# Weight places and prefetch order for the experts of a hybrid decoder layer: seven single gate-up places and a third down place

## The reference, cut to what matters

```
x = x + gate1 * (merged @ w_o)
h = RMSNorm(x) * (1 + scale2) + shift2
# top-1 group of 4, then top-2 of its 8 experts: each token goes to 2 of 32 experts
gate = h @ w_gate[e]          # 1024 x 256 for each expert
up   = h @ w_up[e]            # 1024 x 256
act  = silu(gate) * up * combine[e]
x = x + gate2 * sum_e(act @ w_down[e])     # 256 x 1024
y = RMSNorm(x) * final_norm_w
```

## Time and profile before

| | before |
|---|---|
| median of 3 runs | 1465.02 us (1462.16 to 1473.55) |
| the profiled execution: its own time | 1467.18 us |
| the profiled execution: span of the trace | 1465.4 us |
| granted TensorE clock, mean | 0.949 |
| PE busy | 1346.7 us (92%) |
| DVE busy | 695.8 us (47%) |
| ACT busy | 257.8 us (18%) |
| POOL busy | 146.3 us (10%) |
| bytes moved by DMA | 250.87 MB, mean 171 GB/s |

### The profile page before, as it was taken

The page is one execution under the profiler, slowest core; times in us unless marked ns, Lnnn a source line. Parts: engine busy times, 40 slices in busy tenths (PEclk is TensorE's granted clock), DMA queues, the critical chain, the costliest instruction groups (busy, mean ns, idle before and its releaser), DMA issues. The chain is left out here.

```text
span 1465.4 us, 19419 instructions
## 1 busy us (share of the span) xinstructions
PE 1346.7 (92%) x7097; PEld 968.5 (66%) x7097; DVE 695.8 (47%) x1415; ACT 257.8 (18%) x554; POOL 146.3 (10%) x278
## 2 busy tenths in 40 slices
PE   5999999999999999999989998999999898888784
PEld 2787667788787787676767776788878632222233
DVE  1434677555667675310105566775567611111125
ACT  2201112112222531110112121510001300000001
POOL 0223100000000000222210003000001211111111
PEclk7899999999999999999999997899999888999995
DMA  9463223313313323555561110512236499999945
GB/s 361 155 137 94 98 73 124 121 58 116 115 58 121 103 60 127 180 170 189 187 217 60 41 30 30 219 58 72 86 107 271 187 375 427 424 424 423 409 161 183
DMA packets 61440, 250.87 MB, mean 171 GB/s; under 512 B 10058, under 2 KB 19690, under 8 KB 52234
## 3 DMA queue, kind: packets, MB, share of 16 engines
q1 hardware_dynamic: 40978, 184.26, 34.3%
q10 hardware_dynamic: 10264, 44.97, 8.6%
q0 software_dynamic: 10112, 20.47, 4.1%
HBM read 234.47 MB, written 22.91 MB: 176 GB/s over the span
## 5 line engine op out<-in xcount | busy, mean ns | idle before, releaser
L350 PE MATMUL psum<-arena 128*128 128x272 f32 x1792 | 423.3, 394 | 1.0 <-DVE arena L1903 1.0
L350 PEld LDWEIGHTS psum<-arena 128*128 128x128 f32 x1792 | 339.0, 190 | 80.9 <-issue 6.7
L362 PE MATMUL psum<-arena 128*128 128x272 f32 x1064 | 249.3, 393 | 2.2 <-DVE arena L2078 1.9
L362 PEld LDWEIGHTS psum<-arena 128*128 128x128 f32 x1064 | 199.8, 189 | 51.7 <-issue 9.7
L1255 PE MATMUL psum<-arena 128*128 128x272 f32 x512 | 122.8, 397 | 0.0
L2541 PE MATMUL psum<-arena 128*64 128x512 f32 x512 | 115.6, 603 | 2.7 <-DVE arena L2640 2.7
L1255 PEld LDWEIGHTS psum<-arena 128*128 128x128 f32 x512 | 96.2, 190 | 25.9 <-DVE arena L1380 3.6
L2541 PEld LDWEIGHTS psum<-arena 128*64 128x64 f32 x512 | 35.9, 136 | 71.2 <-issue 71.2
L2562 PE MATMUL psum<-arena 128*64 128x512 f32 x256 | 69.8, 694 | 1.2 <-DVE arena L2629 1.2
L1380 DVE TENSOR_TENSOR arena<-arena,psum 128x272 f32<-128x272 f32 x16 | 7.0, 439 | 132.1 <-ACT arena L1332 123.9
L1574 PE MATMUL psum<-arena 128*128 128x272 f32 x256 | 64.8, 407 | 2.9 <-PEq L206 2.9
(11 more groups left out here) (374 smaller groups left out, 1433.4 us busy)
## 6 DMA issues: line engine op xcount, KB each, us to landing
arena<-in_weights SPq DMA_DIRECT2D x153, 512.0 KB, 4.3
arena<-in_w_gu SPq DMA_DIRECT2D x32, 2048.0 KB, 17.6
arena<-in_w_down ACTq DMA_DIRECT2D x28, 1024.0 KB, 17.2
arena<-in_weights ACTq DMA_DIRECT2D x16, 512.0 KB, 4.1
arena<-in_pages_k POOLq DMA_DIRECT2D x40, 128.0 KB, 3.3
arena<-in_x SPq DMA_DIRECT2D x2, 2176.0 KB, 13.8
arena<-in_pages_v SPq DMA_DIRECT2D x32, 128.0 KB, 3.0
arena<-in_pages_v POOLq DMA_DIRECT2D x32, 128.0 KB, 3.3
```

Of the source, the lines that this page charges most:

```text
L350: mm = pe.matmul(out[:, h, :], lhsT=w_of(n, c), rhs=act[:, c, h * HALF:(h + 1) * HALF], start=(c == 0), stop=(c == DC - 1))
L362: mm = pe.matmul(out, lhsT=w[:, c * P:c * P + P], rhs=x[:, c, :], start=(c == 0), stop=(c == 3))
```

## The change: what it does

- The gate-up weights get seven places for single experts instead of three for pairs. The first six are the halves of the old ones; the seventh is at `a_x`, where `xT` stands. Expert `j` goes to place `j % 7`; from `j` = 7 on it is loaded when `gate_up((j-7)//2)` is done.
- Expert 4 is loaded when the rows have been turned (`s_row_ps`), expert 5 when `h2_rows` is written; neither waits for gather 0 any more.
- `xT` is written to a new DRAM tensor `x_mid` by ACT, behind the last row of `h2_rows` (2176 KB). SP waits for it (`s_xmid`) and for gather 0 and loads expert 6 into its place. Behind `gate_up(13)` SP reads `x_mid` back, and DVE waits for that (`s_xback`) ahead of `residual(0)`.
- The down weights get a third place. All three begin 192 floats lower than before, and pairs 0 and 1 are loaded when `w_o`'s pair `v` = 1 is done instead of `v` = 0, pair 2 by SP behind expert 6. ACT issues pair `p+2` in its step `p` instead of pair `p+1`, behind the same `down(p-1)`.
- Small tables of the router move to addresses that nothing else uses then.

```diff
@@ -2103,16 +2103,19 @@
...
                 "dma_may_start"))
-            gath, scat, wdn_full = (s_gath, s_gath1), (s_scat, s_scat1), (s_wdn, s_wdn1)
-            wgu_full = (s_wgu, s_wgu1, sem("wgu_loaded2"))
-            GU = 3
-            GU_USES = [len(range(k, NP, GU)) for k in range(GU)]
+            gath, scat = (s_gath, s_gath1), (s_scat, s_scat1)
+            wdn_full = (s_wdn, s_wdn1, sem("wdown_loaded2"))
+            GU, DN = 7, 3
+            wgu_full = (s_wgu, s_wgu1) + tuple(sem(f"wgu_loaded{i}") for i in range(2, GU))
+            GU_USES = [len(range(k, 2 * NP, GU)) for k in range(GU)]
+            DN_USES = [len(range(k, NP, DN)) for k in range(DN)]
+            s_xmid, s_xback = sem("x_spilled_and_back"), sem("x_is_back")
+            x_mid = nc.dram_tensor("x_mid", [P, DC, NT], F32).ap()

...
             W_GU = 2 * DC * FF
-            w_gu = [(A.at(a_q, W_GU), A.at(a_q + W_GU, W_GU)), (A.at(a_ring, W_GU), A.at(a_ring + W_GU, W_GU)),
-                    (A.at(a_h, W_GU), A.at(a_w - 192 - W_GU, W_GU))]
-            w_dn = [A.at(a_w, 2, 2 * D), A.at(a_w + 4 * D, 2, 2 * D)]
+            w_gu = [A.at(at, W_GU) for at in (a_q, a_q + W_GU, a_ring, a_ring + W_GU, a_h, a_w - 192 - W_GU, a_x)]
+            w_dn = [A.at(a_w - 192 + 4 * D * k, 2, 2 * D) for k in range(DN)]
             a_e = a_q + 8192
@@ -2159,19 +2162,21 @@
...
             tmp32 = A.at(a_r + 1200, 2, NR, NE)
-            rank = A.at(a_r + 1520, 2 * NR)
+            rank = A.at(a_param + PARAM_AT["conv_prev"][0] + 64, 2 * NR)
             p2 = A.at(a_r + 1530, NR)
             mx = A.at(a_r + 1567, 16)
-            tabf = A.at(a_r + 1583, NP)
-            pick = A.at(a_r + 1600, 2, 2 * NR, NE)
-            slot_of = A.at(a_r + 2240, 2 * NR, CAP)
+            tabf = A.at(a_param + PARAM_AT["conv_prev"][0] + 80, NP)
+            a_dead = a_const + CONST_AT["after"][0]
+            assert a_dead + 4 * NR * NE + 2 * NR * CAP <= a_const + CONST_AT["iota"][0]
+            pick = A.at(a_dead, 2, 2 * NR, NE)
+            slot_of = A.at(a_dead + 4 * NR * NE, 2 * NR, CAP)
             xn11 = A.at(a_r + 2240, DC, NEW)
             pre = A.at(a_r + 2240 + 2 * NR * CAP, NR, NE)
-            wtab = A.at(a_r + 2400 + 2 * NR * CAP, NP)
+            wtab = A.at(a_param + PARAM_AT["conv_prev"][0] + 96, NP)
             wcol = A.at(a_param + PARAM_AT["conv_prev"][0], 2, NR)
...
             rounds_i = A.at(a_keep + 20, 1).bitcast(I32)
-            rows11 = A.at(a_xb + DC * NT - 2 * D, 4, D)
+            rows11 = A.at(a_w - 192 - 4 * D, 4, D)
             assert T_O % RING + 3 < RING and T_END - T_O == RING
@@ -2210,8 +2215,8 @@
...
                     mm.then_inc(w_used, 2)
-                    if v == 0:
-                        pe.wait_ge(w_used, T_O + 2)
+                    if v == 1:
+                        pe.wait_ge(w_used, T_O + 4)
                         pe.sem_inc(s_dn, 2)
@@ -2291,6 +2296,7 @@
...
                     rows_out(i)
+                act.dma_start(x_mid, xT).then_inc(s_xmid, 16)
                 act.wait_ge(s_gi, 1)
@@ -2460,29 +2466,51 @@
...
             def _(sp):
-                def gate_up_in(r, p):
-
-                    sp.wait_ge(s_gu, r * NP + (p if p >= GU else (2, 1, 1)[p]))
+                def gate_up_in(r, j):
+
+                    last = max(k for k in range(j, 2 * NP, GU))
+                    sp.wait_ge(s_gu, r * NP + (3 + (j - GU) // 2 if j >= GU else max(last // 2 + 3 - NP, 1)))
+                    sp.dma_start(w_gu[j % GU], ins["w_gu"][j]).then_inc(wgu_full[j % GU], 16)
+
+                def down_in(r, p):
+                    sp.wait_ge(s_dn, r * NP + (2, 1, 1)[p])
                     for e in range(2):
-                        sp.dma_start(w_gu[p % GU][e], ins["w_gu"][2 * p + e]).then_inc(wgu_full[p % GU], 16)
-
-                def down_in(r, p):
-                    sp.wait_ge(s_dn, r * NP + (p + 1))
-                    for e in range(2):
-                        sp.dma_start(w_dn[p % 2][:, e, :], ins["w_down"][2 * p + e]).then_inc(wdn_full[p % 2], 16)
+                        sp.dma_start(w_dn[p][:, e, :], ins["w_down"][2 * p + e]).then_inc(wdn_full[p], 16)

...
                     gate_up_in(r, 0)
+                    gate_up_in(r, 1)
                     down_in(r, 0)
...
                     sp.wait_ge(w_used, T_END)
-                    gate_up_in(r, 1)
+                    gate_up_in(r, 2)
+                    gate_up_in(r, 3)
+                    sp.wait_ge(s_row_ps, NR)
+                    gate_up_in(r, 4)
+                    for k, n in enumerate((2, 1, 1, 1)):
+                        sp.wait_ge(s_h2w[k], 16 * n)
+                    gate_up_in(r, 5)
                     sp.wait_ge(s_slot, 1)
...
                     sp.wait_ge(gath[0], r * (8 * NP) + 16)
-                    for p in range(2, NP):
-                        gate_up_in(r, p)
+                    sp.sem_inc(s_passed, 1)
+                    sp.wait_ge(s_xmid, r * 16 + 16)
+                    sp.sem_inc(s_passed, 1)
+                    sp.wait_ge(s_sq11, DC)
+                    sp.wait_ge(s_xs, DC - 1)
+                    sp.wait_ge(s_xs7, 1)
+                    sp.wait_ge(s_xn, 1)
+                    gate_up_in(r, 6)
+                    sp.wait_ge(s_wtab, 1)
+                    down_in(r, 2)
+                    for j in range(GU, 2 * NP):
+                        gate_up_in(r, j)
+                    sp.wait_ge(s_gu, r * NP + (3 + max(range(GU - 1, 2 * NP, GU)) // 2))
+                    sp.dma_start(xT, x_mid).then_inc(s_xmid, 16)
+                    sp.wait_ge(s_xmid, r * 16 + 32)
+                    sp.sem_inc(s_passed, 1)
+                sp.sem_inc(s_xback, 1)

@@ -2532,11 +2560,12 @@
...
                     pe.wait_ge(s_xsb, r * NP + (p + 2))
-                    pe.wait_ge(wgu_full[p % GU], r * (32 * GU_USES[p % GU]) + (p // GU * 32 + 32))
+                    for j in (2 * p, 2 * p + 1):
+                        pe.wait_ge(wgu_full[j % GU], r * (16 * GU_USES[j % GU]) + (j // GU * 16 + 16))
                     pe.wait_ge(s_act, r * NP + (p + 1))
...
                         for e in range(2):
-                            wv = w_gu[p % GU][e].rearrange("p (o c f) -> p c o f", o=2, c=DC)
+                            wv = w_gu[(2 * p + e) % GU].rearrange("p (o c f) -> p c o f", o=2, c=DC)
                             at = c * P + CAP * e
@@ -2553,14 +2582,14 @@
...
                     pe.wait_ge(s_asb, r * NP + (p + 1))
-                    pe.wait_ge(wdn_full[k], r * (16 * NP) + (p // 2 * 32 + 32))
+                    pe.wait_ge(wdn_full[p % DN], r * (32 * DN_USES[p % DN]) + (p // DN * 32 + 32))
                     pe.wait_ge(s_yo, r * NP + (p + 1))
...
                                 mm = pe.matmul(psum[CAP * e:CAP * e + CAP, 4 + h, :], lhsT=actT[:, k, at:at + CAP],
-                                               rhs=w_dn[k][:, e, f * D + h * 512:f * D + h * 512 + 512],
+                                               rhs=w_dn[p % DN][:, e, f * D + h * 512:f * D + h * 512 + 512],
                                                start=(f == 0), stop=(f == 1))
@@ -2599,17 +2628,17 @@
...
                 def down_in(r, p):
-                    act.wait_ge(s_dn, r * NP + (p + 1))
+                    act.wait_ge(s_dn, r * NP + p)
                     for e in range(2):
-                        act.dma_start(w_dn[p % 2][:, e, :], ins["w_down"][2 * p + e]).then_inc(wdn_full[p % 2], 16)
+                        act.dma_start(w_dn[p % DN][:, e, :], ins["w_down"][2 * p + e]).then_inc(wdn_full[p % DN], 16)

...
                         act.activation(sil[:, k, :], psum[:, 2 + k, 0:FF], ACT.Silu).then_inc(s_silu12, 1)
-                        if 1 <= p < NP - 1:
-                            down_in(r, p + 1)
+                        if 1 <= p < NP - 2:
+                            down_in(r, p + 2)
                         act.wait_ge(s_aps, r * NP + (p + 1))
@@ -2793,6 +2822,7 @@
...
                 rows_added(4)
+                dve.wait_ge(s_xback, 1)
                 residual(0)
...
                 dve.wait_ge(s_yt, 3)
```

## The result

| | before | changed |
|---|---|---|
| median (11 runs each, same chip) | 1465.51 us | 1482.01 us |
| lowest to highest | 1460.81 to 1473.55 us | 1475.58 to 1485.26 us |
| ratio | | 1.0103, 95% interval 1.0087 to 1.0120 |
| profiled execution: time, span | 1467.18, 1465.4 us | 1485.26, 1483.6 us |

The change costs about 1%, where no change (+5 us) was forecast, and the time lies outside the range.

What follows compares the result with a forecast made beforehand. It took full DMA engines in the expert stage as the bound, reaching PE through gathers. Start +7 and end -2, the rest nothing, gave +5 us on 1465.02, a median of 1470 us; range 1454 to 1478.

Steps and rivals of the forecast that it cites:

- DMA is full and PE waits for gathers: Expert stage: the 16 DMA engines are full, and PE waits for token-row gathers, 35.6 us in 11 waits, not weights.
- Places as depth gain nothing in the pace: Expert stage: seventh place and third down place leave the pace at 16.9 us a pair; costed at nothing.
- The start, 7 us, bounds 0 to 9: Stage start: 6.43 MB ahead of gather 0 makes it land later, so the stage starts 7 us later.
- A late start is carried through unchanged: Expert stage: it repeats itself with the start's shift of 7 us, each trigger keeping its distance to the pairs.
- The way back of `x`: Reading x back behind gate_up(13): needed some 50 us on, so DVE never waits; can only hold up gather 15.
- The end, -2: Last pairs: 5 us less DMA ahead of gather 14 removes turn_x(14)'s 2.46 us wait; -2 us, bounds 0 and -3.5.
- A (turns): Rival at gather 0: engines serve queues in turn, so it lands some 1.3 us later; 1464 us; chance 0.12.
- B: Rival for the stage: bytes moved decide, so filling the gap gains; 1457 us, at most down to 1450; chance 0.19.
- C: Rival from gather 4 on: added places put more in flight, gathers land later; 1485 to 1499 us; chance 0.09.

Runs made afterwards that it cites:

- e4: Kernel before with only POOL's order changed: scatter p-4 instead of p-3 behind gather p, so gathers are issued earlier; ratio 0.9982.
- e7: Against the kernel before: six single gate-up places and three down places, no x out and back, experts 4 and 5 behind gather 0; ratio 1.0050.
- e9: Against the kernel before: six single gate-up places, two down places, gather 0 first, no x out and back; as fast, to 0.04%.
- e11: Changed kernel without the seventh place and without x out and back; early experts 4 and 5 and third down place stay; ratio 1.0049.
- e2: Kernel before in its old places, only expert 4 loaded when rows are turned and expert 5 when they are written; 1479.9 us, ratio 1.0071.
- e3: Changed kernel with expert 4 loaded behind the rows' writes, like expert 5; 1477.6 us.
- e5: Changed kernel with POOL's order changed so that the gather goes ahead of the scatter; 1470.9 us.
- e15: Changed kernel with experts 4 and 5 and the write of x issued behind gather 0's issue, by POOL's semaphore; last down 290.6 us behind w_o's end.
- e1: Changed kernel with experts 4 and 5 and the write of x moved behind gather 0's landing; 1475.8 us.
- e14: Against the kernel before: six gate-up, three down places, gather before scatter, no x, step-11 down load skipped, experts 4 and 5 at gather 0's issue; 1466.1 us, 0.9981.

## Why the prediction was wrong

1. *DMA is full and PE waits for gathers.* Right as a reading: 12 waits for gathers in the changed kernel, none for weights. Wrong as a cause, by e4: remove the gathers' waits and the same 35 us turn up at the down weights.
2. *Places as depth gain nothing in the pace.* Right to 0.2 us in 169. "I cost this at nothing" was wrong for the end: where the start is on time the third down place costs 7.7 us (e7 against e9), through one gather. In e11, which has the early experts and the third down place, its price did not add to the late start's (e11 against e2: 284.1 and 284.3); that the stock is filled while PE waits for gather 0 is the likely reason, not a shown one.
3. *The start, 7 us, bounds 0 to 9.* **This is the step that failed**: measured 11.8, with the rows that expert 4 holds up, and gather 1, put at 2 us together at most, between the 7 and the bound of 9. That the bytes ahead of gather 0 delay it was right, and the sum agrees with e3 (6.9), but in part by luck: by the reading behind it gather 0 would have landed last, and in e3 it landed 3.8 us ahead of expert 5. I counted all 6.43 MB as flowing from 1164 on, "since whatever of it goes earlier pushes bytes of the rows behind it". What was missed: expert 5 and gather 0 are issued on the landing of these rows, and expert 4, with `x` behind it, held the last block up by 8 us (10.8 instead of 2.8; without `x`, in e2, 7.9), so gather 0 was issued 6.4 us later. Transfers that are chained by a landing don't share a sum of bytes. Taking expert 4 away from the rows gives 4.9 us back (e3).
4. *A late start is carried through unchanged.* Right to 0.9 us: 11.8, 10.9, 11.0. It holds only while PE waits for gathers: with the gather ahead, 10.4 us at the start are 3.9 at the end (e5).
5. *The way back of `x`.* Landed 12.5 us behind its issue, no wait of DVE: right.
6. *The end, -2.* Wrong in sign: from `gate_up(13)` to the last `down` 43.8 us, before 42.3. Expert 31 alone in the queue did not help gather 14, which took about as long as before and kept its wait (2.32), now with a slow `down` behind it (5.35 us).

By its own terms the sum should have been 11.8 + 0.7 = 12.5 instead of 5 (0.7 is the end's 1.5 less the 0.8 that the shift lost on the way to pair 13). Its upper bound has a slip of 1 us: 1465 and 9 are 1474, not 1475. The medians differ by 16.5 in the first measurement, and by 13 to 14 if the later medians of the kernel before are taken; the trace explains 12.5, and whether the rest is more than the choice of runs stays open.

Of the rivals, A (turns) is refuted for the time that it gave: gather 0 took some 9.6 us in the changed kernel, 11.0 in e3 and 15.4 in e15, where 5.5 was its price; but gathers that land ahead of older loads (e3) say that there is something to it. The Trainium skill's rule behind it (DMA: Bandwidth & Descriptors, Queues, rings and completion order, round-robin by packets) may hold inside the engines, but a landing can't be priced from it. The same section says that an engine's completion increment lands only after all its earlier writes, across its queues; the landings in e15 fit that (the gather 1.6 us behind `x`), and no run isolates it. B had the right premise, bytes set the pace, and the wrong conclusion, since bytes moved into the gap opened another. C's sign came true by another mechanism: gathers 4 to 13 landed no later (the odd ones, which the trace has, in 22.4 to 24.9 us, and 22.5 to 25.5 before).

What stays open: why e1, with `x` beside the first pair and 4.2 MB of depth, ends 7.3 us late like e7 without `x`. PE waits for gate-up weights there (12.9 us, and 4.5 more that the profile puts down to "issue") and for gathers (30.1), and no run separates `x`'s bytes from the depth.

## What to carry to other kernels

A gap in the transfers just ahead of a small transfer on which the compute waits is no free room: price what is put there by when that small transfer lands, and follow each issue that is chained to a landing. In a stage whose DMA is full, find out with one reordering whether the transfer waited for is the cause or only the last; if the wait moves to another transfer with its sum unchanged, bytes are the bound; here no other order and no other number of places brought more than 0.2%. Look at the last trip as well as at the pace: stock that nobody waited for was paid there in e7.

## What the runs showed of the hardware

- A gather of some 0.28 MB: 4.2 us on idle queues, 7.7 us (e2) to 15.4 us (e15) beside 2 to 6 MB, 23 us beside the full stage. The last row write, 128 KB, behind a 2 MB load on another queue: 7.9 us (e2) instead of 2.8, and 10.8 with the write of `x` behind it on its own queue (the changed kernel).
- Order of issue is not order of landing: in e3 the gather was issued 2.5 us after expert 5 on another queue and landed 3.8 us ahead of it.
- A semaphore that POOL increments behind its indirect DMA did not put other transfers behind that DMA: in e15 the transfers that wait for it were issued at 1166.4 and 1166.5, and the gather's record starts at 1166.58; in e14 the first load was 0.1 us ahead as well.
- A wait of PE of 5.0 us cost 7.6: in the work behind it the granted clock was 0.50 (e7). The Trainium skill (TensorE: Matmul & The Clock Gate, Part 1) describes the two levels, 1.2 and 2.4 GHz; the granted 0.50 agrees.
